# Sums of squares added up on VectorE ahead of single products, an input load that goes first, and a prepared table and clock

## The reference, cut to what matters

```
# first block (16 meta tokens are put in front: 272 tokens)
xn   = rmsnorm(h, g_mix_pre);  proj = xn @ w_in            # q, k, v, r, gate, u, two z
o    = rmsnorm(gla_chunked(q, k, v, log_a), gla_norm_g) * silu(r)   # per head of 256
y    = sigmoid(z_gla) * (o @ w_o_gla) + sigmoid(z_ssm) * glu(gelu(s5_ssm(u)))
h    = h + rmsnorm(y @ w_out, g_mix_post)                  # norm 2
f    = square(relu(rmsnorm(h, g_ffn_pre) @ w_ff1)) @ w_ff2 # norm 3
h    = h + rmsnorm(f, g_ffn_post)                          # norm 4
# second block
h    = h + concat(mlstm, window attention)(rmsnorm(h, g_mix)) @ w_out     # norm 5
h    = h + cross_attention(rmsnorm(h, g_cross), rmsnorm(mem, g_mem))      # norms 6 and 1
h    = h + peer_ffn(rmsnorm(h, g_ffn))                     # 16 of 16384 experts per head
out  = rmsnorm(h, g_final)

rmsnorm(x, g) = x * rsqrt(mean(x * x) + 1e-6) * g
```

## Time and profile before

| | |
|---|---|
| median of 3 runs | 1533.63 us (1533.52 to 1534.07) |
| profiled execution | 1534.28 us |
| its span, first to last instruction | 1532.5 us |
| PE busy | 1267.4 us (83%) |
| DVE busy | 962.0 us (63%) |
| ACT busy | 345.1 us (23%) |
| POOL busy | 507.2 us (33%) |
| mean granted TensorE clock | 0.907 of full speed |

### The profile page before, as it was taken

One profiled execution on the slowest core, in us unless ns is written; L12 is line 12 of the kernel. 1 busy time (PEld: TensorE's weight loads), 2 busy tenths in 40 slices (PEclk: granted clock), 3 DMA queues, 4 the chain that ended last, 5 costly groups with the idle time before them and its releaser, 6 DMA issues.

```text
span 1532.5 us, 14639 instructions
## 1 busy us (share of the span) xinstructions
PE 1267.4 (83%) x5246; PEld 910.3 (59%) x5246; DVE 962.0 (63%) x1854; ACT 345.1 (23%) x703; POOL 507.2 (33%) x406
## 2 busy tenths in 40 slices
PE   7999999999999999999999996666656555666554
PEld 5776778888888888887888884222222212222221
DVE  6899985142310000324422498999998998989877
ACT  2543433221100000123302412111111211111111
POOL 3367771010000000000010255666554545555550
PEclk9999999999999999999999999777787788767787
DMA  6232333243344444333363499999999999999995
GB/s 247 98 111 83 110 115 133 100 179 138 137 148 154 155 148 162 139 111 110 110 241 134 179 421 409 418 422 422 421 421 422 421 422 421 422 421 421 422 421 214
DMA packets 55167, 390.16 MB, mean 255 GB/s; under 512 B 6208, under 2 KB 6528, under 8 KB 8384
## 3 DMA queue, kind: packets, MB, share of 16 engines
q0 software_dynamic: 38256, 276.58, 43.5%
q1 hardware_dynamic: 15840, 110.24, 20.3%
q10 hardware_dynamic: 1008, 2.52, 0.4%
HBM read 388.27 MB, written 1.05 MB: 254 GB/s over the span
## 4 chain that ended last, share of the span: by engine, by line
PE 58%; DMA 17%; DVE 16%; POOL 4%; issue 2%; ACT 2%; ACTq 0%; DVEq 0%
PE psD L971 16%; DMA ring<-in_expert,arena 12%; PE psD L919 8%; PE psD L1017 7%; PE psD L402 7%; DMA arena<-in_expert,arena 5%; PE psD L990 4%; POOL arena L2026 2%; DVE arena L2039 2%; DVE ring L2039 2%; PE psD L1575 2%; PE psB L1858 2%; DVE feat L2073 2%; DVE feat L2039 2%; PE psD L1348 2%
## 5 line engine op out<-in xcount | busy, mean ns | idle before, releaser
L971 PE MATMUL psD<-feat,ring 128*128 128x256 f32 (+1 forms) x1120 | 248.7, 383 | 3.7 <-DVE feat L356 3.2
L971 PEld LDWEIGHTS psD<-feat,ring 128*128 128x128 f32 x1120 | 214.0, 192 | 34.7 <-issue 4.5
L2026 POOL DMA_INDIRECT feat<-in_expert,arena x77 | 110.1, 1430 | 187.4 <-DVE arena L1996 164.0
L2026 POOL DMA_INDIRECT arena<-in_expert,arena x102 | 131.3, 1288 | 105.4 <-DVE arena L1996 69.0
L2242 POOL DMA_DIRECT2D feat<-in_xo x3 | 1.7, 553 | 446.9 <-PE psN L332 446.9
L2039 DVE CUSTOM_DVE_ANT_0 arena<-arena,feat 128x1024 f32<-128x1024 f32 x102 | 121.6, 1222 | 29.1 <-DMA arena<-in_expert,arena 29.0
L1858 PE MATMUL psB<-arena 128*128 128x512 f32 x128 | 84.3, 819 | 59.1 <-ACT arena L1928 59.1
L919 PE MATMUL psD<-feat,ring 128*128 128x256 f32 (+1 forms) x576 | 132.2, 387 | 0.0
L919 PEld LDWEIGHTS psD<-feat,ring 128*128 128x128 f32 x576 | 107.8, 190 | 24.0 <-issue 7.8
L402 PE MATMUL psD<-feat,ring 128*128 128x256 f32 x512 | 110.8, 379 | 0.0
L1017 PE MATMUL psD<-feat,ring 128*128 128x256 f32 x512 | 110.7, 379 | 0.0
(11 more groups left out here) (542 smaller groups left out, 2166.5 us busy)
## 6 DMA issues: line engine op xcount, KB each, us to landing
ring<-in_w SPq DMA_DIRECT2D x103, 1024.0 KB, 4.8
feat<-in_xo POOLq DMA_DIRECT2D x3, 1024.0 KB, 7.7
arena<-in_expert,arena POOLq DMA_INDIRECT x102, 22.5
feat<-in_expert,arena POOLq DMA_INDIRECT x77, 18.8
feat<-in_xT SPq DMA_DIRECT2D x2, 544.0 KB, 4.3
arena<-in_w_akv POOLq DMA_DIRECT2D x1, 1024.0 KB, 5.4
feat<-in_memT POOLq DMA_DIRECT2D x1, 1024.0 KB, 5.9
VT<-in_xo POOLq DMA_DIRECT2D x1, 1024.0 KB, 11.6
```

What stands on the lines that cost most here:

```text
L971: mm = nc.tensor.matmul(psD[:, 2 * (c % 2) + m, 0:T], ring[:, c % RING, k, m * P:(m + 1) * P], x[:, k], start=(k == 0), stop=(k == KT - 1))
L2026: (nc.gpsimd.indirect_dma_start(GPAIR[b], None, a["expert"], bass.IndirectOffsetOnAxis(ap=EID[:, t, c:c + 1], axis=0)) .then_inc(s_gb[b], 16))
```

## The change

1. **Norm 1.** A new function `memory_squares_dve` adds the 8 blocks on VectorE in three linked steps (4, 2 and 1 blocks), ahead of norm 1's scaling; `memory_sums_pe` makes one product.
2. **Heads.** VectorE adds the two blocks of each head, 128 tokens at a time; TensorE makes one product for each head.
3. **Norms 2, 4 and 6.** VectorE also adds blocks 6, 7 and then block 1 onto block 0; TensorE makes one product. Norms 3 and 5 (`PARTED`) keep their four products. All waits on `s_sqa` are counted anew.
4. **Place.** The sums of norms 2 and 4 move from ahead of the first chunk of `xk0` and `xk1` to behind its fifth product (`place=5`); the others keep their place.
5. **Start, loads.** SyncE asks for `xT`, waits until both halves have landed, and then asks for `cols`, two ring slots, the six inputs that ScalarE asked for before, and the other two ring slots.
6. **Start, table and clock.** `s_const` is raised once when `ones` is filled and once at the old place. ScalarE squares one column of `ones` as soon as it has asked for its three inputs, which makes it load its table; TensorE makes 8 products of `ones` with itself ahead of norm 0.

```
+    PARTED = (3, 5)
+    def memory_squares_dve(link):
+        nc.vector.wait_ge(s_sqm, 2)
+        for n in (4, 2, 1):
+            ins = nc.vector.tensor_tensor(SQ[:, 0:n, 0:T2], SQ[:, 0:n, 0:T2], SQ[:, n:2 * n, 0:T2], ALU.add)
+            if n > 1:
+                link(ins)
+        ins.then_inc(s_sqa, 1)
...
     def memory_sums_pe():
-        for k in range(KT):
-            if k % 4 == 0:
-                nc.tensor.wait_ge(s_sqm, k // 4 + 1)
-            mm = nc.tensor.matmul(psN[:, 0:T2], ones[:, :], SQ[:, k, 0:T2], start=(k == 0), stop=(k == KT - 1))
-        mm.then_inc(s_ms, 1)
+        nc.tensor.wait_ge(s_sqa, 3)
+        nc.tensor.matmul(psN[:, 0:T2], ones[:, :], SQ[:, 0, 0:T2], start=True, stop=True).then_inc(s_ms, 1)
...
     def squares_dve(i, link):
-        for j in (1, 2):
+        for j in (1, 2) if i in PARTED else (1, 2, 3):
...
+        if i not in PARTED:
+            ins = nc.vector.tensor_tensor(SQ[:, 0, 0:T2], SQ[:, 0, 0:T2], SQ[:, 1, 0:T2], ALU.add)
         ins.then_inc(s_sqa, 1)
...
+        nc.tensor.wait_ge(s_sqa, i + 2)
+        blocks = (0, 1, 6, 7) if i in PARTED else (0,)
...
     def gla_pe_norm():
-        nc.tensor.wait_ge(s_osq, 2)
+        nc.tensor.wait_ge(s_sqa, 2)
         for h in range(GH):
-            for m in range(2):
...
     def gla_dve_norm(link):
-        nc.vector.wait_ge(s_osq, 2)
+        pairs = SQ.rearrange("p (h m) t -> p h m t", m=2)
+        for g in range(2):
+            nc.vector.wait_ge(s_osq, g + 1)
+            v = pairs[:, :, :, g * P:(g + 1) * P]
+            nc.vector.tensor_tensor(v[:, :, 0], v[:, :, 0], v[:, :, 1], ALU.add).then_inc(s_sqa, 1)
...
+                if mid and m * KT + k == place:
+                    mid()
...
+        for i in range(2):
+            sp.wait_ge(s_x[i], 16)
+        sp.dma_start(cols[:, :], a["cols"]).then_inc(s_cols, 16)
+        for j in range(2):
+            load(j, j)
+        sp.dma_start(walow[:, :, :], a["w_alow"]).then_inc(s_small, 16)
...
+        for j in range(2, RING):
             load(j, j)
...
-        g.memset(ones[:, :], 1.0)
+        g.memset(ones[:, :], 1.0).then_inc(s_const, 1)
...
+        act.activation(RT[:, 0, 0:1], ones[:, 0:1], ACT.Square)
...
+        for i in range(8):
+            pe.matmul(psN[:, 0:P], ones[:, :], ones[:, :], start=True, stop=True)
...
-        sums_pe(2)
-        chunk_pe(FIRST["xk0"], 0, MEM, T2, fresh=2)
+        chunk_pe(FIRST["xk0"], 0, MEM, T2, fresh=2, mid=lambda: sums_pe(2), place=5)
```

More of the change, by code:

```diff
@@ L327, in sums_pe @@
         nc.tensor.wait_ge(s_rt, i)
-        nc.tensor.wait_ge(s_sqa, i - 1)
-        for k in (0, 1, 6, 7):
+        nc.tensor.wait_ge(s_sqa, i + 2)
+        blocks = (0, 1, 6, 7) if i in PARTED else (0,)
+        for k in blocks:
             if k == 6:
                 nc.tensor.wait_ge(s_sqp, 4 * (i - 2) + 4)
-            mm = nc.tensor.matmul(psN[:, 0:T2], ones[:, :], SQ[:, k, 0:T2], start=(k == 0), stop=(k == 7))
+            mm = nc.tensor.matmul(psN[:, 0:T2], ones[:, :], SQ[:, k, 0:T2], start=(k == 0), stop=(k == blocks[-1]))
         mm.then_inc(s_ms, 1)
@@ L958, in drain, with chunk_pe @@
         drained[0] = max(drained[0], upto)
-    def chunk_pe(first, j, x, T, fresh=None, ready=None, clear=None, mid=None):
+    def chunk_pe(first, j, x, T, fresh=None, ready=None, clear=None, mid=None, place=KT):
         c = first + j
@@ L2155, in _ @@
             sp.dma_start(H[:, 4 * i:4 * i + 4], a["xT"][:, 4 * i:4 * i + 4]).then_inc(s_x[i], 16)
-        sp.dma_start(cols[:, :], a["cols"]).then_inc(s_cols, 16)
         w = a["w"]
@@ L2162, in load @@
                          ).then_inc(s_w[j], 16)
-        for j in range(RING):
+        for i in range(2):
[4 more added lines that the diff above has]
+        sp.dma_start(walow[:, :, :], a["w_alow"]).then_inc(s_small, 16)
+        sp.dma_start(wgu[:, :], a["w_gate_up"]).then_inc(s_small, 16)
+        sp.dma_start(BR, a["b_re"]).then_inc(s_s5b, 16)
+        sp.dma_start(BI, a["b_im"]).then_inc(s_s5b, 16)
+        sp.dma_start(CM[0], a["c_re"]).then_inc(s_s5c, 16)
+        sp.dma_start(CM[2], a["c_im"]).then_inc(s_s5c, 16)
+        for j in range(2, RING):
             load(j, j)
@@ L2399, in _ @@
             dve.tensor_tensor(RRB[:, v], RRB[:, v], UUB[:, v], ALU.add).then_inc(s_mix, 1)
+        memory_squares_dve(link)
         prenorm_dve(1, MEM, "g_mem_2", MEM, link)
@@ L2479, in _ @@
         ff2_pe(FFH, T2)
-        sums_pe(4)
-        chunk_pe(FIRST["xk1"], 0, MEM, T2, clear=FIRST["w_ff2"] + 12)
+        chunk_pe(FIRST["xk1"], 0, MEM, T2, clear=FIRST["w_ff2"] + 12, mid=lambda: sums_pe(4), place=5)
         chunk_pe(FIRST["xk1"], 1, MEM, T2, mid=lambda: sums_pe(5))
```

18 lines of the change are left out of this document (5 added, 13 removed).

## The result

The changed kernel takes 1527.86 us (median of 6 runs, 1526.97 to 1529.36); the kernel before, run on the same chips, 1533.85 us (6 runs). The ratio is 0.9962, 95% interval 0.9952 to 0.9972: 6.0 us faster, between 4.3 and 7.4. The forecast was 8.9 us and 1524.7 us; the range ended at 1527.5. Its direction is right; it comes 2.9 us short of the size forecast, and lies outside the range.

A forecast was written before the change was run, and what follows sets the result against it. PE, busy 83% of the span, was taken as the bound, with gathers setting the late pace. Terms 2.9 + 1.7 + 3.0 + 0 + 0 + 1.3 = 8.9 us off 1533.63 gave 1524.7 us; 8-in-10 range 1522.2 to 1527.5.

The forecast's parts named there:

- the bounds given: Norms 2 and 4 with the waits at norms 3 and 5: gain 0 each, from -0.4 to 1.3 us.
- Rival 2: Residual not rigid behind the root: norms 2 and 4 keep 1.3 us each, 1522.1 us; chance 9%.
- rival 1: Weights late at the start: ring slots land about 24 us, 6.4 us lost, 1534.0 us in all; chance 3%.
- term A: The start: norm 0's reciprocal on DVE at 12.2 instead of 15.12 us, gain 2.9 us, bounds 1.5 and 3.5.
- rival 4: One stretch at 1.2 GHz more or less on the scan's chain: 1526.9 or 1522.5 us; chance 14%.

The follow-up runs named there:

- three products: The whole changed kernel with norms 2 and 4 made of three products (blocks 0, 6 and 7) behind the chunk's first product: 1527.34 us, ratio 0.9957.
- norms alone: The kernel before with only the changes of the norms and heads, start as before: 1529.37 us, ratio 0.9972.
- cut before: The kernel before, ended behind norm 2's residual, all that follows left out: median 405.69 us.
- cut norms: The kernel before with only the changes of the norms and heads, ended behind norm 2's residual: median 401.90 us.
- start alone: The kernel before with only the changes of the start, norms as before: 1532.96 us, ratio 0.9997.
- cut start: The kernel before with only the changes of the start, ended behind norm 2's residual: median 406.71 us.
- cut after: The changed kernel, ended behind norm 2's residual, without a chunk of xk0 around norm 2's product: median 400.98 us.

## Why the prediction missed

**Right.** The heads gave 1.72 and norm 1 3.02 us in the profiles, with no new wait. For norms 2 to 5 I had said that the saving comes back as a wait at norms 3 and 5 of 1.0 to 1.4 us and the gain is 0; the wait is 1.34 at each and the balance -0.3, inside the bounds given. The delay of the root was 0.89, not 0.77, since norm 2's one product took 0.56 us and not 0.43. Norm 6 gave 1.12 of 1.3, since PE stood 0.3 us ahead of its product where I had nothing. Rival 2 is out (the residual is rigid, and three products win by it), and so is rival 1: no wait of PE for a ring load. The gathers' stage is as long as before. Together the norms were sized at 6.0 and gave 5.3.

**Wrong: term A, the start, sized at 2.9 us, with 1.5 as its lowest.** The step that failed is the sum "Reciprocal at 12.2; gain 2.9 us" and the premise that it passes to the end, since "everything behind it hangs on it": the reciprocal came 1.9 us earlier in the mean and not 2.9, and what it won was lost again, in three of five profiles, by a stretch at the lower clock near 50 us. Four readings of what the start is worth are 0.5 (alone), 1.5 (after less norms alone), 0.9 and -1.0 (cut, with and without the norms): about 0.5. Its steps one by one, from these profiles (us; an execution each):

| profile | sums start, us long | reciprocal | first chunks, us long | scan's first products | stretches at 0.50, to 57 us |
|---|---|---|---|---|---|
| before | 7.92, 6.54 | 15.12 | 17.79 | 52.59 | 16.7 (6.8) |
| norms alone | 8.05, 6.32 | 15.04 | 14.90 | 51.98 | 36.8 (3.4) |
| cut before | 7.97, 5.29 | 13.92 | 16.59 | 50.40 | 17.6 (3.4) |
| cut norms | 7.95, 6.10 | 14.72 | 14.90 | 51.15 | 36.3 (3.4) |
| after | 5.63, 5.70 | 13.34 | 16.59 | 50.07 | 16.1 (3.4), 50.2 (6.8) |
| start alone | 5.92, 3.93 | 12.63 | 17.93 | 50.24 | 14.5 (6.8) |
| cut start | 5.90, 3.93 | 12.63 | 16.55 | 48.87 | 15.1 (3.4), 49.2 (6.8) |
| cut after | 5.92, 3.93 | 12.63 | 17.86 | 50.18 | 14.3 (6.8) |
| three products | 6.01, 3.93 | 12.64 | 16.39 | 48.91 | 14.8 (3.4), 48.9 (6.8) |

1. *The base.* I took 15.12 from the one trace there was. It was the latest of four; their mean is 14.70. 0.4 us of the 2.9 were never there to win.
2. *The end.* I took 12.2; the last five profiles of the table have 12.63 or 12.64 four times and 13.34 once, mean 12.8. "With cols and weights held back `log_step` can land up to 1 us earlier" failed: VectorE started at 6.29 us in the mean of these five, against 6.49 in the mean of the four before. Most of its work ahead of the reciprocal hangs on that landing, and behind it the sums and the root's table load lie close. 0.6 us.
3. *The clock.* Reciprocal and scan's first products both come 1.9 us earlier in the mean (14.70 to 12.77, 51.53 to 49.65). Then the low stretch near 50 us takes it back in three of these five profiles. Its price can be read exactly, since the chain behind is rigid: from the scan's first products to VectorE's fourth step in the scan (105.41 us in before, 106.21 in after) it is 52.8 us in each of the 16 profiles without that stretch, 56.1 in each of the three with 6.8 us of it, and 54.5 in the one with 3.4. So it costs 3.3 us each time, 2.0 in the mean of the five. I had a stretch more or less as rival 4, at 2.2 us either way and at 132.7 us. Its price was wrong in both places: 3.3 near 50, and 0.4 at 132.7, where I had read PE's MATMULs as the chain and VectorE's step takes most of it up.

2.9 less 0.4, 0.6 and 2.0 is -0.1. So in the mean of these nine profiles nothing of the start is left at 105 us: VectorE's fourth step stands at 104.36 with the old start and at 104.47 with the new one. The four readings by times, about 0.5, agree within what they can tell. The shares of 1 and 2 rest on nine profiles; the third is less sure. None of the four profiles of the old start has the stretch near 50 us, three of five of the new one have it, and so has the one without opening products; not the ones with the earlier table or with the loads as before, and none of eight with products held there. That is too few to say that the frequency differs. Two of the five times of the cut norms (403.56, 404.00 against 401.54 to 401.90) are long too; the stretch near 50 would do that, but so would what before's profile shows, 1.4 us at the scan's first products (52.59 against the 51.15 of the cut norms' own profile) and 0.4 at 132.7. Settled is what the stretch costs when it comes; how often it comes, and whether the new start brings it, stays open.

The Trainium skill (TensorE: Matmul & The Clock Gate, section Part 1: The HAM clock gate) says that the point where the clock rises differs from run to run; the table agrees: the same 16 MATMULs behind the same opening products took 3.93 or 5.70 us. I had cited it for the reciprocal alone; in these profiles the low stretches behind it, at 33 to 37 and near 50 us, differ from one to the next as well.

The queues came out well. The first two ring slots landed at 11.6 and 14.3 us, where the forecast had 11 and 13.5. `cols` landed 1.7 us after its request, `w_alow` 6.9, `w_gate_up` 7.6, `b_re` 8.0, `b_im` 8.7, `c_re` 9.5 and `c_im` 10.5, in the order of the requests, and PE never waited for the ring. The Trainium skill (DMA: Bandwidth & Descriptors, section Queues, rings and completion order) has each DMA engine take the descriptors of one queue in ring order, and these landings agree.

One slip in the forecast's reading: it says that the granted clock stands at nine tenths "for 28 slices and falls only in the last twelve". The earlier trace rows shows 25 and 15. And the 1.00 that it sets against PE's pace at 10.9 us is no record: in that trace the record of the clock begins at 13.25 us. No term hangs on either.

## What to carry to other kernels

Before a gain at a kernel's start is sized from one trace, look for how much of the base is chance: the start of this kernel, a phase with idle gaps of TensorE, put one reciprocal 1.2 us apart in four profiles, and the shorter sums made the gap behind them longer (3.20 us before, 4.54 after). Price a stretch at the lower clock by what sets the pace where it falls: the same 6.8 us cost 3.3 us beside TensorE's chain and 0.4 beside VectorE's. Ask of each engine when it would be free if the bound went away; here VectorE's own work, the slow sums and the root lay within half a microsecond, so that removing one gave little. A sum that others wait for should come early rather than be short: three products right away beat one product behind two additions.

## What the runs showed of the hardware

- Two waits ahead of an ACTIVATE that needs another table: one stands on the table load, and if it is the late one, 1.28 us come into the open (11.42 in after, 15.31 with the old loads). With one wait the load stood under the sums, at 8.79 in before, and with the other wait moved ahead of the second squares at 7.32.
- Products that only keep PE busy weren't free: 16 of 128 columns (32 MATMULs) took 3.73 us, from 45.36 to 49.1. With the gap behind norm 0 filled by such products the clock fell at 33 and 34 us instead, but it fell at 34 to 37 us in four profiles without them too.
- From the scan's first products to VectorE's fourth step, 52.81 to 52.83 us in 16 profiles: executions differ by where the clock is low, and by nothing else there.
- A 0.2 KB load took 4.3 us to land as third in its queue beside the input, and 1.8 us when it was asked for first.
